# A hybrid encoder trunk on one core: four passes with one sequence's mixers laid between the other's feed-forward matmuls

## The chip, the core and the metric

The kernel runs on one core of one Trainium2 chip. Its metric is the device time in microseconds. TensorE does the matmuls and transposes, VectorE and ScalarE the elementwise work, and SyncE issues the DMAs; GpSimd has no part in it. Each engine works through its own list of instructions in order and waits on semaphores.

## The reference, cut to what matters

Two layers act on two sequences of 512 tokens of width 1024 (`x_prompt` and `x_sample`, with the same weights).

```
def encoder_layer(x, ...):
    h = rms_norm(x, norm_mix_g)
    proj = h @ w_in                       # 2864 columns
    aq, ak, av, bq, bk, bv, bg, ba, cq, ck, cv, co, cg = split(proj)
    attn = axial_gqa_attention(...)       # 8 heads of 64, 2 key heads, rotary, softmax over 512 keys
    gla = gla_mixer(...)                  # 4 heads, both directions, decay per channel
    mls = mlstm_mixer(...)                # 4 heads, both directions, gates with a running maximum
    x = x + concatenate([attn, gla, mls]) @ w_out
    u = centred_dwconv(rms_norm(x, norm_ffn_g) @ w_up, conv_w, conv_b)   # 3 taps over tokens, 5632 columns
    gate, val = split(u)
    return x + (silu(gate) * val) @ w_down                               # 2816 rows
```

## The kernel before, in words

Features lie on partitions and tokens on the free axis: `x` is [128, 8, 1024] for both sequences together. Every operand of a projection is split into a rounded part and its remainder (`whi` and `wlo`, `hh` and `hl`, `acth` and `actl`), and `passes3` (lines 433 to 435) issues three matmuls for each product. The dense work comes in units of weights of [128, 1024], 512 KB. SyncE loads a unit into `raw`, ScalarE writes `whi` (lines 820 and 1050), VectorE subtracts and writes `wlo` (lines 1149 and 1608). A unit serves both sequences.

One loop runs over the two layers. In a layer the stages follow each other:

- The norm: squares, their sum over partitions by a matmul with ones (line 417), root, reciprocal, the spreading over partitions (line 425), then eight rows for each sequence (`hf` line 1179, `hh` line 842, `hl` line 1183).
- The input projection of 23 units: 14 with tokens on the output's partitions (128x256 outputs), 9 with features there (128x512). Its results are moved by ScalarE and VectorE by turns, and rotary work of the queries and keys lies between.
- The mixers of both sequences. Queries and keys are split and transposed. In attention each of 64 steps has scores (lines 529 and 530), the row maximum (`nmx`, 1285), the exponential with its sum (906), four transposes (540), the copy of these (`pT`, by VectorE and ScalarE in turns, 1293 and 927), and the product with the values (551), with a hand-written shift of two and three steps. Three banks hold scores, three hold outputs, two hold transposes. The gates of linear attention (Abs, Exp, Ln; bias line 899) are put among the steps. Linear attention then goes chunk by chunk (32 tokens): states (582, 1472), scores (596), outputs (614, 620), with the backward direction's gates and the mLSTM's gate rows laid between its chunks. The mLSTM has 8 heads (4 for each sequence): row terms (669) in two banks, key-query products (678, 679) in four, decays (1008, 1012), products (1559), values (695) and a division (1526 to 1537).
- The output projection of 8 units, with `x` loaded back from memory, and then the second norm.
- The feed-forward: a loop over 22 tiles `j` of the inner width. For each, a gate unit and a value unit are multiplied for both sequences (96 matmuls of 128x512), ScalarE gives the middle tap with bias, VectorE adds the outer taps (1618, 1621), Silu and product (1075, 1645), split (1089, 1648), and the down unit of `j - 1` adds 16 products of 128x512 to `x` (line 1630).

```
                    pe.wait_ge(g_conv, j)
                    up(0, j)
                    pe.wait_ge(v_conv, j)
                    up(1, j)
                    down(j - 1, first=first)
```

The order of each engine's work is this written order alone; there is no planner. A mixer's memory shares regions with the weights' splits, with `hh` and `hl` and with `x`, so no mixer can run beside a projection.

## Time and profile before

| what | value |
| --- | --- |
| time, median of 3 runs | 3286.31 us (3283.18 to 3289.34) |
| span of the profiled execution, from first to last instruction | 3279.8 us |
| its device time beyond the span | not recorded apart; the median lies 6.5 us above the span |
| instructions | 41387 |
| mean granted TensorE clock | 0.907 of full speed |
| busy: TensorE, its weight loads, VectorE, ScalarE | 89%, 74%, 58%, 29% |

A share of busy time is an average over stages with different limits. Time in a stage is read from a window of the trace, and the clock column says at what part of full speed TensorE was let run there. The busy time of matmuls is modelled at its end, so the number of matmuls in a window is the firmer figure.

### The profile page before, as it was taken

To read this page: it belongs to the slowest core of one execution; us is meant where nothing else is said; L and a number is where in the kernel's file an instruction comes from. 1 tells how busy PE (TensorE), PEld (TensorE's weight loads), DVE (VectorE), ACT (ScalarE), POOL (GpSimd) and SP (SyncE) were. 2 spreads that over 40 slices of the span, in tenths; PEclk is the share of its full clock that TensorE was granted. 3 is DMA by queue.
4 is the path that set the end of the run, shared out by engine and by line. 5 is a ranking of instruction groups with operands and counts; after the bars stand their busy time and mean duration, and the time that the engine had idled before them with its cause. 6 is when DMAs were issued, how large, how long until landed. Compare 5 with 4: busy or idle time off the path is not lost.

```text
span 3279.8 us, 41387 instructions
## 1 busy us (share of the span) xinstructions
PE 2919.6 (89%) x16292; PEld 2435.9 (74%) x16292; DVE 1914.4 (58%) x2737; ACT 939.7 (29%) x1457; POOL 0.2 (0%) x4
## 2 busy tenths in 40 slices
PE   6999878778799999999889988797697999999997
PEld 6987766567688787878679867665676878788785
DVE  5532775664466666576646236756635675666666
ACT  3112641343222222222221145414323222222222
POOL 0000000000000000000000000000000000000000
PEclk9999985579899999999989999755698999999998
DMA  4110000002011111111121100000020111111111
GB/s 170 50 48 17 1 1 1 7 1 104 13 58 38 57 39 41 55 38 58 58 76 39 53 9 1 1 1 7 1 104 33 39 39 57 38 58 38 54 42 58
DMA packets 35624, 131.55 MB, mean 40 GB/s; under 512 B 4196, under 2 KB 5732, under 8 KB 35244
## 3 DMA queue, kind: packets, MB, share of 16 engines
q1 hardware_dynamic: 35500, 129.82, 11.3%
q8 instruction: 88, 1.44, 0.2%
q14 instruction: 36, 0.29, 0.0%
HBM read 117.22 MB, written 12.58 MB: 40 GB/s over the span
## 4 chain that ended last, share of the span: by engine, by line
PE 82%; DVE 10%; issue 4%; ACT 3%; DMA 1%; SPq 0%; DVEq 0%; ACTq 0%; PEldq 0%
PE ps L433 22%; PE ps L435 22%; PE ps L434 21%; PE ps L695 3%; PE ps L551 3%; PE ps L614 2%; PE ps L620 1%; DVE x L1630 1%; PE ps L582 1%; PE ps L540 1%; DVE sqsum L1120 1%; PE ps L678 1%; PE ps L529 1%; PE ps L679 1%; PE ps L530 1%
## 5 line engine op out<-in xcount | busy, mean ns | idle before, releaser
L433 PE MATMUL ps<-hh,wlo 128*128 128x512 f32 x1952 | 769.5, 394 | 61.0 <-PE ps L435 38.3
L435 PE MATMUL ps<-hh,whi 128*128 128x512 f32 x1952 | 762.0, 390 | 0.0
L434 PE MATMUL ps<-hl,whi 128*128 128x512 f32 x1952 | 761.6, 390 | 0.0
L1630 DVE TENSOR_TENSOR x<-x,ps 128x512 f32<-128x512 f32 x704 | 482.4, 688 | 284.9 <-PE ps L435 284.7
L433 PEld LDWEIGHTS ps<-hh,wlo 128*128 128x128 f32 x1952 | 367.3, 188 | 170.5 <-issue 94.0
L435 PEld LDWEIGHTS ps<-hh,whi 128*128 128x128 f32 x1952 | 367.4, 188 | 77.8
L434 PEld LDWEIGHTS ps<-hl,whi 128*128 128x128 f32 x1952 | 367.7, 188 | 73.6
L433 PE MATMUL ps<-acth,wlo 128*128 128x512 f32 x704 | 280.7, 399 | 17.0 <-DVE actl L1648 14.3
L435 PE MATMUL ps<-acth,whi 128*128 128x512 f32 x704 | 278.2, 395 | 0.0
L433 PE MATMUL ps<-whi,hl 128*128 128x256 f32 x896 | 256.6, 286 | 24.0 <-DVE wlo L1149 20.3
L434 PE MATMUL ps<-actl,whi 128*128 128x512 f32 x704 | 276.0, 392 | 0.0
L434 PE MATMUL ps<-wlo,hh 128*128 128x256 f32 x896 | 255.4, 285 | 0.0
L435 PE MATMUL ps<-whi,hh 128*128 128x256 f32 x896 | 255.3, 285 | 0.0
L1050 ACT ACTIVATE whi<-raw 128x1024 fp32r<-128x1024 f32 x132 | 138.7, 1054 | 398.2 <-PEq L757 380.8
L433 PEld LDWEIGHTS ps<-whi,hl 128*128 128x128 f32 x896 | 173.9, 194 | 28.5 <-DVE wlo L1149 22.7
L1618 DVE SCALAR_TENSOR_TENSOR accg<-ps,cw,accg 128x1022 f32<-128x1022 f32 x44 | 56.4, 1282 | 232.8 <-ACT accg L1068 232.8
L434 PEld LDWEIGHTS ps<-wlo,hh 128*128 128x128 f32 x896 | 173.9, 194 | 0.0
L435 PEld LDWEIGHTS ps<-whi,hh 128*128 128x128 f32 x896 | 173.8, 194 | 0.0
L433 PEld LDWEIGHTS ps<-acth,wlo 128*128 128x128 f32 x704 | 133.7, 190 | 47.4 <-issue 15.1
L1608 DVE TENSOR_TENSOR wlo<-raw,whi 128x1024 fp32r<-128x1024 f32 x132 | 160.5, 1217 | 11.6 <-ACT whi L1050 11.6
L551 PE MATMUL ps<-tokA,pT 128*128 128x64 f32 x1024 | 141.0, 283 | 27.2 <-ACT pT L927 27.1
L551 PEld LDWEIGHTS ps<-tokA,pT 128*128 128x128 f32 x1024 | 130.8, 200 | 36.5 <-ACT pT L927 33.7
(212 smaller groups left out, 3645.5 us busy)
## 6 DMA issues: line engine op xcount, KB each, us to landing
raw<-d_w_ffn SPq DMA_DIRECT2D x132, 512.0 KB, 4.9
raw<-d_w_units SPq DMA_DIRECT2D x62, 512.0 KB, 3.9
d_x_out<-x SPq DMA_DIRECT2D x24, 512.0 KB, 2.6
x<-d_x_out SPq DMA_DIRECT2D x2, 4096.0 KB, 13.6
x<-d_x_in SPq DMA_DIRECT2D x8, 512.0 KB, 7.8
mR<-d_sel SPq DMA_DIRECT2D x2, 400.0 KB
w2s<-d_w2p SPq DMA_DIRECT2D x2, 256.0 KB, 2.6
cmask<-d_chunkmask SPq DMA_DIRECT2D x1, 256.0 KB, 3.0
```

The costliest lines, as they stand in the source:

```text
L433: pe.matmul(out, stat[1], mov[0], start=first, stop=False)
L434: pe.matmul(out, stat[0], mov[1], start=False, stop=False)
L435: return pe.matmul(out, stat[0], mov[0], start=False, stop=last)
L529: pe.matmul(ps[:, 3 + i % 3, :], q, ks[:, 1, h // 4, keys], start=True, stop=False)
L530: pe.matmul(ps[:, 3 + i % 3, :], q, ks[:, 0, h // 4, keys], start=False, stop=True).then_inc(sc_ready, 1)
L551: mm = pe.matmul(ps[:, v % 3, 0:HD], pT[:, v % 2, kt, :], tokA[:, s * SB + kt, c0:c0 + HD], start=(kt == 0), stop=(kt == SB - 1))
L614: mm = pe.matmul(ps[:, bank, cols], attT[:, i % 2, h % 2, h // 2, :], gv[:, tt, h * HD:(h + 1) * HD], start=True, stop=False, skip_group_c ...
L695: mm = pe.matmul(ps[:, 6 + d, j * (HD + 1):(j + 1) * (HD + 1)], Dts[w % 2][:, d, i, j * P:(j + 1) * P], vaug[:, s * SB + i, h, :], start=( ...
L1050: act.activation(whi[:, kind, :, :], raw[:, kind, :].rearrange("p (k c) -> p k c", k=KT), ACT.Copy).then_inc(f_hi[kind], 1)
L1608: dve.tensor_tensor(wlo[:, kind, :, :], raw[:, kind, :].rearrange("p (k c) -> p k c", k=KT), whi[:, kind, :, :].bitcast(F32), ALU.subtract ...
L1618: dve.scalar_tensor_tensor(acc[:, :, 1:SEQ], ps[:, pair:pair + 2, 0:SEQ - 1], cw[:, taps:taps + 1], acc[:, :, 1:SEQ], ALU.mult, ALU.add).t ...
L1630: dve.tensor_tensor(xs, xs, ps[:, 4 + o % 2 * 2 + s, :], ALU.add).then_inc(d_done, 1)
```

## The change

The kernel is written anew around one sequence at a time. A *pass* is a layer of a sequence: passes 0 and 1 are layer 0 of the two sequences, 2 and 3 layer 1. Each pass has its own input projection (23 units), mixers, output projection (8 units) and feed-forward (66 units), and each unit is loaded and split anew in every pass; `whi` has four slots and `wlo` and `raw` six. The order is: norm of sequence 0; projection 0; mixers 0 alone; output projection 0; then for p = 1, 2, 3 the projection of p, the feed-forward of p - 1 with the mixers of p between its matmuls, and the output projection of p; last, norm and feed-forward of pass 3. The other norms lie beside projections: their squares, sum, root, spreading and rows are handed out over the units of an input projection, or over the eight units of the output projection of passes 1 and 2.

The feed-forward of a pass is a list of 132 slots. Up units have two slots of 12 matmuls, a pair of down units four slots of 12. All engines go through the same list, and `steps_after` puts one of 114 mixer steps behind nearly every slot, from slot 1 to slot 125. The feed-forward keeps to PSUM banks 0 to 3 and the mixers to 4 to 7. So attention has two banks of scores, one of transposes and one of outputs, and all copies of transposes are ScalarE's. The output of four query tiles is scaled by one operation. An mLSTM head has one bank for row terms and one for key-query products. Linear attention's states are formed as products of all chunks first, and then a chain of 30 operations for each direction on VectorE; both directions' outputs are added in PSUM. Silu is replaced by Tanh of half the argument, x(1 + tanh(x/2)), with the factor one half in the value's taps. Evacuations of the input projection are all ScalarE's. All loops over layers and tiles are unrolled.

```diff
-                def iteration(j, first=False):
-                    pe.wait_ge(g_conv, j)
-                    up(0, j)
-                    pe.wait_ge(v_conv, j)
-                    up(1, j)
-                    down(j - 1, first=first)
-                iteration(1, first=True)
-                with pe.Fori(2, FT) as j:
-                    iteration(j)
-                down(FT - 1, last=True)
...
+FF_SLOTS = []
+for _jj in range(FF_PAIRS + 1):
+    if _jj < FF_PAIRS:
+        FF_SLOTS += [("up", 2 * _jj, 0, 0), ("up", 2 * _jj, 0, 1), ("up", 2 * _jj, 1, 0), ("up", 2 * _jj, 1, 1)]
+    if _jj >= 1:
+        FF_SLOTS += [("down", _jj - 1, 0, o) for o in range(SB)]
+    if _jj < FF_PAIRS:
+        FF_SLOTS += [("up", 2 * _jj + 1, 0, 0), ("up", 2 * _jj + 1, 0, 1),
+                     ("up", 2 * _jj + 1, 1, 0), ("up", 2 * _jj + 1, 1, 1)]
...
+MIX_STEPS = [("qk", tt) for tt in range(SB + 1)]
+MIX_STEPS += [("att", i) for i in range(N_ATT + 3)]
...
+def steps_after(slot):
+    n = len(MIX_STEPS)
+    return MIX_STEPS[min(slot, MIX_SPAN) * n // MIX_SPAN:min(slot + 1, MIX_SPAN) * n // MIX_SPAN]
...
+            def feed_slot(f, n):
+                kind, j, which, half = FF_SLOTS[n]
+                hh, hl = R_at[f % NSEQ]["hh"], R_at[f % NSEQ]["hl"]
+                if kind == "up":
+                    u = UNIT_AT[("up", f, j, which)]
+                    if half == 0:
+                        pe.wait_ge(lo_ready, u + 1)
+                        if j == 0:
+                            pe.wait_ge(h_ready, h_count(f)[1])
+                            if f + 1 < N_PASS:
+                                pe.wait_ge(proj_evac, E_ALL * (f + 1) + 33 + which)
+                        else:
+                            pe.wait_ge((g_conv, v_conv)[which], FT * f + j)
+                    for k in range(half * 4, half * 4 + 4):
+                        mm3 = passes3(ps[:, which, :], (whi[:, HI[u], k, :], wlo[:, LO[u], k, :]),
+                                      (hh[:, k, :], hl[:, k, :]), k == 0, k == KT - 1)
+                    if half == 1:
+                        mm3.then_inc(up_done, 1)
+                else:
+                    if half == 0:
+                        pe.wait_ge(lo_ready, UNIT_AT[("down", f, 2 * j + 1, 2)] + 1)
+                        pe.wait_ge(actl_ready, FT * f + 2 * j + 2)
+                        if j == 0 and f + 1 < N_PASS:
+                            pe.wait_ge(proj_evac, E_ALL * (f + 2))
+                    for o in (2 * half, 2 * half + 1):
+                        if j or o >= 2:
+                            pe.wait_ge(d_done, FF_ADDS * f + KT * j + o - 1)
+                        for m in range(2):
+                            u = UNIT_AT[("down", f, 2 * j + m, 2)]
+                            mm3 = passes3(ps[:, 2 + o % 2, :], (whi[:, HI[u], o, :], wlo[:, LO[u], o, :]),
+                                          (acth[:, m, :], actl[:, m, :]), m == 0, m == 1)
+                        mm3.then_inc(d_psum, 1)
...
+            def attention(p, i):
+                rb, xb = R_at[p % NSEQ], X_at[p % NSEQ]
+                at = N_ATT * p
+                if i < N_ATT:
+                    h, qt = i // SB, i % SB
+                    if i == 0:
+                        pe.wait_ge(qkT_act, 2 * SB * (p + 1))
+                        pe.wait_ge(qkT_dve, SB * (p + 1))
+                        pe.wait_ge(z_taken, SB * (p + 1))
+                    if i >= 2:
+                        pe.wait_ge(prob_ready, at + i - 1)
+                    q = rb["qs"][:, h, qt * P:(qt + 1) * P]
+                    pe.matmul(ps[:, 4 + i % 2, :], q, rb["ks"][:, 1, h // 4, :], start=True, stop=False)
+                    pe.matmul(ps[:, 4 + i % 2, :], q, rb["ks"][:, 0, h // 4, :], start=False,
+                              stop=True).then_inc(sc_ready, 1)
+                if 2 <= i < N_ATT + 2:
+                    v = i - 2
+                    pe.wait_ge(prob_ready, at + v + 1)
+                    if v >= 1:
+                        pe.wait_ge(pT_ready, at + v)
+                    for kt in range(SB):
+                        tr = pe.transpose(ps[:, 6, kt * P:(kt + 1) * P], xb["prob"][:, v % 3, kt * P:(kt + 1) * P],
+                                          ident[:])
+                    tr.then_inc(pT_psum, 1)
+                if i >= 3:
+                    v = i - 3
+                    pe.wait_ge(pT_ready, at + v + 1)
+                    if v >= SB and v % SB == 0:
+                        pe.wait_ge(ao_done, AH * p + v // SB)
+                    c0 = AV + v // SB // 4 * HD
+                    for kt in range(SB):
+                        mm = pe.matmul(ps[:, 7, v % 4 * HD:(v % 4 + 1) * HD], xb["pT"][:, v % 2, kt, :],
+                                       tokA[:, kt, c0:c0 + HD], start=(kt == 0), stop=(kt == SB - 1))
+                    mm.then_inc(ao_psum, 1)
...
+                if i >= 2:
+                    kt = i - 2
+                    pe.wait_ge(stk_lo, 3 * (at + w + 1))
+                    if w or kt:
+                        pe.wait_ge(wt_ready, 8 * (at + w) + 2 * kt)
+                    k = xb["ks2"][:, w % 2, kt * P:(kt + 1) * P]
+                    pe.matmul(ps[:, 5, :], k, xb["ql2"][:, w % 2, :], start=True, stop=False)
+                    pe.matmul(ps[:, 5, :], k, xb["qh2"][:, w % 2, :], start=False, stop=True).then_inc(qk_psum, 1)
...
+            for p in range(N_PASS):
+                q = side_norm(p, "in")[0]
+                for i in range(N_IN):
+                    if i == 6:
+                        sum_squares(q)
+                    if i == 10:
+                        spread(q)
+                    project(p, i)
+                if p == 0:
+                    for step in MIX_STEPS:
+                        mix_step(p, step)
+                else:
+                    for n in range(len(FF_SLOTS)):
+                        feed_slot(p - 1, n)
+                        for step in steps_after(n):
+                            mix_step(p, step)
+                beside = side_norm(p, "out")
...
+                    split_to(first + (3 if kind == "up" else 3))
+                if kind == "up" and half == 1:
+                    at = FT * f + j
+                    act.wait_ge(up_done, FF_UPS * f + 2 * j + which + 1)
+                    if which == 0:
+                        if at:
+                            act.wait_ge(act_ready, at)
+                        act.activation(accg[:], ps[:, 0, :], ACT.Identity, bias=convs[:, l, j, 3:4],
+                                       scale=convs[:, l, j, 1:2]).then_inc(g_init, 1)
+                        act.wait_ge(g_conv, at + 1)
+                        act.activation(sil[:], accg[:], ACT.Tanh, scale=0.5).then_inc(sil_ready, 1)
+                    else:
+                        if at:
+                            act.wait_ge(actl_ready, at)
+                        act.activation(accv[:], ps[:, 1, :], ACT.Identity, bias=convs[:, l, j, 7:8],
+                                       scale=convs[:, l, j, 5:6]).then_inc(v_init, 1)
+                        if j % 2 or j == 0:
+                            round_act(f, j)
+                if kind == "down" and half == 3 and j + 1 < FF_PAIRS:
+                    round_act(f, 2 * j + 2)
+            def round_act(f, j):
+                act.wait_ge(act_ready, FT * f + j + 1)
+                if j >= 2 or f:
+                    act.wait_ge(d_psum, FF_ADDS * f + KT * (j // 2))
+                act.activation(acth[:, j % 2, :], accv[:], ACT.Copy).then_inc(acth_ready, 1)
...
+            def attention(p, i):
+                rb, xb = R_at[p % NSEQ], X_at[p % NSEQ]
+                at = N_ATT * p
+                if i < N_ATT:
+                    act.wait_ge(nmx_ready, at + i + 1)
+                    if i >= 3:
+                        act.wait_ge(pT_psum, at + i - 2)
+                    act.activation(xb["prob"][:, i % 3, :], ps[:, 4 + i % 2, :], ACT.Exp, bias=nmx[:, i:i + 1],
+                                   accum_out=rsum[:, i:i + 1]).then_inc(prob_ready, 1)
+                if 2 <= i < N_ATT + 2:
+                    v = i - 2
+                    act.wait_ge(pT_psum, at + v + 1)
+                    if v >= 2:
+                        act.wait_ge(ao_psum, at + v - 1)
+                    act.activation(xb["pT"][:, v % 2, :, :].rearrange("p k q -> p (k q)"), ps[:, 6, :], ACT.Copy)\
+                       .then_inc(pT_ready, 1)
...
+            def feed_slot(f, n):
+                kind, j, which, half = FF_SLOTS[n]
+                l = f // NSEQ
+                x = X_at[f % NSEQ]["x"]
+                if half == 0:
+                    first = UNIT_AT[("up", f, j, which) if kind == "up" else ("down", f, 2 * j, 2)]
+                    split_to(first + 3)
+                if kind == "up" and half == 1:
+                    at = FT * f + j
+                    if which == 0:
+                        conv(accg, 0, convs[:, l, j, 0:4], g_init, g_conv, at)
+                    else:
+                        conv(accv, 1, convs[:, l, j, 4:8], v_init, v_conv, at)
+                        dve.wait_ge(sil_ready, at + 1)
+                        link(dve.scalar_tensor_tensor(accg[:], sil[:], 1.0, accg[:], ALU.add, ALU.mult))
+                        dve.wait_ge(v_conv, at + 1)
+                        dve.tensor_tensor(accv[:], accg[:], accv[:], ALU.mult).then_inc(act_ready, 1)
+                        if j % 2 or j == 0:
+                            rest_of_act(f, j)
+                if kind == "down":
+                    for o in (2 * half, 2 * half + 1):
+                        dve.wait_ge(d_psum, FF_ADDS * f + KT * j + o + 1)
+                        dve.tensor_tensor(x[:, o, :], x[:, o, :], ps[:, 2 + o % 2, :], ALU.add).then_inc(d_done, 1)
+                    if half == 3 and j + 1 < FF_PAIRS:
+                        rest_of_act(f, 2 * j + 2)
+            def rest_of_act(f, j):
+                dve.wait_ge(acth_ready, FT * f + j + 1)
+                dve.tensor_tensor(actl[:, j % 2, :], accv[:], acth[:, j % 2, :].bitcast(F32), ALU.subtract)\
+                   .then_inc(actl_ready, 1)
...
+                for m in (range(8) if part == 0 else range(8, 15)):
+                    c = m if d == 0 else NCH - 1 - m
+                    for hp in range(2):
+                        own = ps[:, 4 + c % 4, (c // 4 * 2 + hp) * HD:(c // 4 * 2 + hp + 1) * HD]
+                        if m == 0:
+                            ins = dve.tensor_copy(st[:, hp, c, :], own)
+                        else:
+                            dve.wait_ge(state_ready, at + 2 * m + hp - 1)
+                            before = c - 1 if d == 0 else c + 1
+                            ins = dve.scalar_tensor_tensor(st[:, hp, c, :], st[:, hp, before, :],
+                                                           aL[:, d, hp, c:c + 1], own, ALU.mult, ALU.add)
+                        ins.then_inc(state_ready, 1)
...
+                        dve.wait_ge(dt_ready, 8 * (at + w))
+                    dve.tensor_tensor(xb["mR"][:, d, :].rearrange("p (j t) -> p j t", j=SB),
+                                      ps[:, 4, :].rearrange("p (j t) -> p j t", j=SB),
+                                      mmask[:, d:d + 1, :].to_broadcast([P, SB, P]), ALU.add).then_inc(mr_ready, 1)
+                if w < MH and i == 2 and w + 1 < MH:
+                    stack_lo(p, w + 1)
+                if w >= 1 and i == (2 if w < MH else 1):
+                    divide(p, w - 1)
+                if i >= 2:
+                    kt = i - 2
+                    Dt = R_at[p % NSEQ]["Dt"][w % 2]
+                    dve.wait_ge(qk_psum, SB * (at + w) + kt + 1)
+                    for d in range(2):
+                        lo, hi = fwd_or_bwd_range(d, kt)
+                        dve.wait_ge(rb_used, 2 * (at + w + 1))
+                        dve.wait_ge(dt_ready, 8 * (at + w) + 2 * kt + d + 1)
+                        D_t = Dt[:, kt, decay_at(d, lo, hi)]
+                        dve.scalar_tensor_tensor(D_t, ps[:, 5, lo:hi], HD ** -0.5, D_t, ALU.mult,
+                                                 ALU.mult).then_inc(wt_ready, 1)
```

In the diff the first functions `feed_slot`, `attention` and the end of `mlstm_head` are TensorE's; the next `feed_slot` with `round_act` and `attention` are ScalarE's; the last ones VectorE's. `stack_lo` writes the three remainders of the next head, `divide` is the division of the head before. ScalarE splits the unit three ahead at the first half of a slot's unit, and VectorE does so too.

## Rows read from the trace of the kernel before

**Rows 1.** The page: busy time of TensorE and others, then its clock in 40 slices.

```profile
...
PE 2919.6 (89%) x16292; PEld 2435.9 (74%) x16292; DVE 1914.4 (58%) x2737; ACT 939.7 (29%) x1457; POOL 0.2 (0%) x4
...
PEclk9999985579899999999989999755698999999998
...
```

**Rows 2.** Windows: length, busy us of PE, PEld, DVE, ACT, POOL, clock, DMA, GB/s.

```profile
...
0.00:34.50 34.50, 6.94 (x20) 4.66 (x20) 16.80 (x21) 14.94 (x16) 0.20 (x4) 0.94 0.80 303
34.50:304.90 270.40, 265.74 (x1776) 244.58 (x1776) 105.70 (x140) 46.10 (x72) 0.00 (x0) 0.99 0.14 47
304.90:763.00 458.10, 352.72 (x2780) 294.24 (x2781) 302.53 (x598) 210.76 (x429) 0.00 (x0) 0.74 0.01 4
329.50:470.00 140.50, 125.79 (x896) 111.84 (x896) 97.00 (x236) 82.88 (x179) 0.00 (x0) 0.95 0.00 1
470.00:624.00 154.00, 117.44 (x1280) 90.33 (x1280) 96.12 (x141) 33.18 (x38) 0.00 (x0) 0.51 0.00 1
655.00:661.60 6.60, 5.36 (x17) 4.51 (x18) 6.50 (x14) 2.42 (x7) 0.00 (x0) 0.50 0.00 0
763.00:851.50 88.50, 86.49 (x374) 69.15 (x372) 22.48 (x21) 12.91 (x13) 0.00 (x0) 1.00 0.23 90
851.50:896.40 44.90, 28.79 (x116) 21.07 (x117) 32.67 (x43) 17.18 (x25) 0.00 (x0) 0.86 0.07 24
900.00:1600.00 700.00, 685.18 (x2985) 558.77 (x2984) 446.61 (x511) 158.00 (x166) 0.00 (x0) 1.00 0.13 46
...
```

**Rows 3.** Timeline of TensorE in one attention step: start, us, instruction.

```profile
...
384.56 0.48 PE L529 MATMUL ps<-ks,qs 128*128 128x512 f32 x1
...
385.11 0.60 PE L540 MATMUL ps<-ident,prob 128*128 128x128 f32 x4
...
386.36 0.48 PE L529 MATMUL ps<-ks,qs 128*128 128x512 f32 x1
...
```

**Rows 4.** Groups of the feed-forward and norms, by shape: busy us, mean ns, idle before.

```profile
...
L1630 DVE TENSOR_TENSOR x<-x,ps 128x512 f32<-128x512 f32 x704 | 482.4, 688 | 284.9 <-PE ps L435 284.7
...
L1608 DVE TENSOR_TENSOR wlo<-raw,whi 128x1024 fp32r<-128x1024 f32 x132 | 160.5, 1217 | 11.6 <-ACT whi L1050 11.6
...
L1050 ACT ACTIVATE whi<-raw 128x1024 fp32r<-128x1024 f32 x132 | 138.7, 1054 | 398.2 <-PEq L757 380.8 <-DMA raw<-d_w_ffn 16.6
...
L1179 DVE SCALAR_TENSOR_TENSOR hf<-x,vec,ps 128x512 f32<-128x512 f32 x64 | 47.1, 746 | 16.8 <-DMA vec<-d_vecs 9.0 <-PE ps L425 6.2
...
L842 ACT ACTIVATE hh<-hf 128x512 fp32r<-128x512 f32 x64 | 40.5, 632 | 71.1 <-DVE hf L1179 70.9
...
L899 ACT ACTIVATE G<-ps,vec 128x512 f32<-128x512 f32 x16 | 11.0, 689 | 4.7 <-PE ps L497 4.7
...
```

**Rows 5.** Groups of the attention steps, by shape.

```profile
...
L906 ACT ACTIVATE prob<-ps,nmx 128x512 f32<-128x512 f32 x128 | 87.9, 687 | 108.8 <-DVE nmx L1285 108.7
...
L927 ACT ACTIVATE pT<-ps 128x512 f32<-128x512 f32 x64 | 37.7, 588 | 3.3 <-PE ps L540 3.3
L1319 DVE TENSOR_SCALAR tokA<-ps,rinvp 128x64 f32<-128x64 f32 x128 | 36.3, 283 | 66.9 <-PE ps L551 62.6 <-DVE rinvp L1296 0.9
...
L906 ACT ACTIVATION_READ_ACCUMULATOR prob<-ps,nmx 128x1 f32 x128 | 24.8, 194 | 0.0
...
L906 ACT ACT_TABLE_LOAD x6 | 7.7, 1283 | 0.1
...
```

**Rows 6.** Timeline of an mLSTM head: start, us, instruction, idle before and its releaser.

```profile
...
656.24 0.76 PE L678 MATMUL ps<-ql,ks 128*128 128x512 f32 x1 [3.05 <-DVE Dt L1559]
...
665.31 0.17 DVE L1526 COPY dn<-ps 128x8 f32<-128x8 f32 x1 [3.59 <-PE ps L695]
...
667.34 0.42 DVE L1537 TENSOR_TENSOR co<-co,hs 128x256 f32<-128x256 f32 x1
...
672.18 4.57 PE L695 MATMUL ps<-vaug,Dt 128*128 128x65 f32 x40
...
```

2420 lines of the change are left out of this document (1158 added, 1262 removed).

## The prediction

> **What bounds the kernel now.** I read the page first. TensorE is busy for 89% of the span and its granted clock is full or nearly so but for one stretch in each layer [rows 1]. So I cut one layer into stages [rows 2]: the input projection, 270.4 us, the mixers, 458.1, the output projection, 88.5, the norm before the feed-forward with its first loads, 44.9, and 700 us of the feed-forward. Its 3168 matmuls at the 700/2985 us of that row are 743, so of half the span, 1640, some 80 are left for norms. What the reader is to see is the clock column. Projections and feed-forward hold 0.99 to 1.00 with TensorE busy for 98% of the time; there only fewer matmuls could help. The mixers hold 0.74 on average, and the gated-linear-attention stretch 0.51. So 458 us a layer, 916 in all, run without the dense matmuls, and the norms are 160 more. That is all that overlap can win from.
>
> **What the change does to each part.** Matmuls of the projections and of the feed-forward keep their number. The change works on one sequence of 512 at a time, in four passes. Mixers of passes 1 to 3 lie beside the feed-forward of the pass before; those of pass 0, one norm and the last feed-forward stay alone. The price is twofold: each weight unit is loaded and split four times, not twice (388 for 194), and all engines now run one common list of 132 slots with 114 mixer steps laid in, each engine in order.
>
> *Loads.* 194 more units of 512 KB add some 100 MB to 130 over the whole run; the feed-forward moves 46 GB/s now and the start 303 [rows 2]. The ring loads five or six units ahead, so I cost it at nothing. Splits: 194 times 1.05 us on ScalarE and 1.22 us on VectorE [rows 4]. In the projections they lie beside matmuls. Beside mixers they don't, see below.
>
> *Start to dense projection*: 34.5 now [rows 2]; half the squares, but each of 8 rows of the norm paces the first tile: 32. *Projections*: four passes of half the row, 4 x 135.2 = 541. *Output projections*: 4 x 44.25, and 1 us each for the last adds: 181. *Last norm*, for one sequence: 8 squares summed (8 x 0.69), root and spreading (some 6), 8 rows of two VectorE operations of 0.69 to 0.75: 25, of 44.9 now.
>
> *Mixers of pass 0, alone.* Half of 458 would be 229. But the new list has one bank where there were three or several, so chains are serial. Attention: a score needs the probability two steps before, whose copy comes behind an exponential on ScalarE: 0.69 + 0.19 + 0.59 (ScalarE), 1.3 (transposes and values on TensorE), 0.7 (scores), 0.69 (maximum, VectorE's price for 512 columns) for two steps, 4.3 with handovers, 2.15 each as now (140.5/64) [rows 2 to 5]: 35 steps 75, gates 10. Query and key transposes 21. Linear attention 85 (half of the row is 77, the rest is its single chain). Norms and gate rows 29, that were laid in it before. mLSTM heads 19 each, 76: splits, division and the first products stand one behind another on VectorE. Last norm and mix 12. Together 308.
>
> *One slot of the passes 1 to 3.* Twelve 128x512 matmuls at 685.18/2985 = 0.23 us [rows 2] are 2.75 us; 132 slots 363. Mixers add per sequence: attention 1.80 a step (384.56 to 386.36 [rows 3]), 32 of them 58; heads 4 x 7 = 28 (40 matmuls of values 4.57 [rows 6]); linear attention some 35 (half of 117.44, which ran at clock 0.51); the rest 16: 137. The bound from the other side is half of the 352.7 us that the mixers were busy, 176 [rows 2]. TensorE's floor for a pass is thus 500 us. VectorE: 66 splits of 1.22, 88 adds of 0.69, 88 convolution steps of 0.75, 66 products and remainders of 0.69 [rows 4]: 252, and half the mixers' 302.5 is 151 [rows 2]: 403. So neither engine is full; what costs is order.
>
> *The waits, by chain.* (a) At the end of an odd value unit VectorE and ScalarE must do, in this order: bias 0.69, two convolutions 1.5, two products 1.4, rounding 0.63, remainder 0.69, then the maximum 0.69, exponential with its sum 0.88, and the copy 0.59 [rows 4, 5]. With 0.05 for each of nine handovers, 0.16 from the slot's last issue to the matmul's end (my estimate), and ScalarE 0.4 late from the step before, that is 8.1 us after the slot's matmuls. TensorE gets to the transposes that need this copy after 1.80 + 2.75 + 0.55 = 5.1. It waits 3.0. (b) After an even value unit the same chain without rounding: 1.2. (c) The adds of the down projection stand behind (b) and a split; its third product needs the first add: 1.5, and 3.1 where no mixer step lies between. Over the twelve slots of two j: 12 x 4.55 = 54.6 and 5.7 of waits, 60.3, 5.0 a slot. (d) In the heads, step 2 puts on VectorE a split 1.22, the next head's remainders 3 x 0.69, the division 2.45 (665.31 to 667.76) and the first products 1.0, behind a ScalarE that is late itself; TensorE's next key-query product has one bank and needs them [rows 6]. I get 6 to 7 us of idle per head, and 31.5 per head against 23.5 of matmuls. In the kernel before the like of it is seen once a head, 3.05 idle [rows 6].
>
> *The clock.* That idle time of 3.05 at 653 to 656 is followed by a granted clock of 0.50 from 655.0 to 661.6 [rows 2, 6]: the next matmuls run at 1.2 GHz, not 2.4. Waits (a), (d) and the 3.1 of (c) are as long. I take 2 us for each; in the feed-forward of before there were no such waits, and it held 1.00.
>
> *Sum of a pass's slots*: queries and keys 5 slots, serial, 38; attention 35 x 5.0 + 4 empty slots 11 + gates and scans 8 + clock 2 = 196; preparation and state chains, 26 slots, 104 (VectorE 84 and its waits, in lumps of 8 us: 60 operations of 0.28 [rows 5]); output tiles 5 slots, 43; norms and gate rows 13 slots, 45; heads 4 x 31.5 + 2 more steps 8 + 3 empty slots 8 + clock 4 = 146; last norm and mix 35; the 7 other slots with the last activation's chain 27. Sum 634, 134 over the floor. Both ends: no wait at all, 500; all waits half as long again and a slower clock after each, 690.
>
> *Last feed-forward*: 363, ten waits (c) of 3.1 and their clock 2 each, 51, first and last chain and store 11: 425. (Before, half of 743: 372.)
>
> Total: 32 + 541 + 308 + 181 + 3 x 634 + 25 + 425 = 3414, against a span of 3279.8. The median of the runs lies 6.5 us above that span; with it, 3420. The removed 916 of mixers and 160 of norms come back as 308, 25, three times 271 of mixer matmuls and waits, and 62 in the last feed-forward, 1208 in all.
>
> For Tanh, which takes the place of Silu beside the exponentials, no row shows which functions share a table; I add no load. The Trainium skill (ScalarE: Activation LUTs, "Table sets: the hidden batching unit") lists tanh in the set of exp, which would keep these loads away; no run here shows it yet.
>
> **Rivals.**
> 1. *The streams interleave cleanly (faster).* ScalarE and VectorE have 30% and more of idle time in a pass, and where a wait is long the engines behind catch up. With fixed parts of 1512 the kernel is faster once a pass's slots take under (3280 - 1512)/3 = 589 us, so if the waits are under 89 rather than 134. At 530 it gives 3110. For it: in the feed-forward of before VectorE was busy for 64% and TensorE lost only 2% [rows 2]. Against: the heads before waited 3 us each, with more banks.
> 2. *A clock that never settles (much slower).* The mixers' windows at 0.51 and 0.74 have shown that many small matmuls with idle time between hold the clock low [rows 2]. If the slots see a clock of 0.85, a pass takes 690: 3590. Against: the attention stretch, busy for 90%, held 0.95.
> 3. *Tanh and Exp each load a table.* A load is 1.28 us [rows 5]; two for each of 22 units in 3 passes are 170 us of ScalarE, on chain (a): some 120 more, 3540. A profile with some 130 more loads would show it.
> 4. *Nothing comes of it*: the gain of the overlap and the price of waits and splits cancel, 3280.
>
> The Trainium skill describes rival 2 (TensorE: Matmul & The Clock Gate, "A second HAM failure mode: psum-queue depth-cycling"): short idle times at each change of PSUM banks make the clock swing, even in dense kernels. By it also the 1 us waits would tell. The trace agrees only for the 3 us ones: from 900 to 1600 us, with a bank handover in every unit, it is 1.00.
>
> **Chances.** Forecast 0.56, rival 1 0.22, rival 2 0.12, rival 3 0.06, rival 4 0.04. A difference of 0.2% is about what a measurement can tell here. Faster 0.22, same 0.04, slower 0.74. Time 3420; the likeliest case alone reaches from 3330 to 3500. The range takes in half of rival 1 and the near part of rival 2: 3180 to 3580.
>
> **What would show it.** Right: 400 or so splits of each kind; TensorE's busy share down to about 80% or less outside the projections; idle of about 3 us before the probability transposes once in two j, of 5 and more before the key-query products, both released by VectorE or ScalarE; clock 0.9 to 0.95 in the slots; each pass's slots 590 to 690 us; pass 0's mixers about 308 us. Wrong: slots under 589 us with waits of 1 us and less (rival 1), or pass 0's mixers near 230, so that my serial chains are too long; a clock near 0.85; table loads in the hundreds.

## Result and the profile after

The changed kernel takes **3430.93 us** (median, 3430.12 to 3435.4), the kernel before 3287.82 beside it: a ratio of 1.0447, interval 1.0429 to 1.0464. It is 143 us slower. The forecast was 3420.

The page of the changed kernel has these lines in answer to [rows 1], and the chain that ended last:

```profile
span 3429.1 us, 39998 instructions
...
PE 2888.8 (84%) x16272; PEld 2398.8 (70%) x16272; DVE 1892.1 (55%) x2821; ACT 1260.2 (37%) x2014; POOL 0.2 (0%) x4
...
PEclk9985579999988899989989899999999889899999
...
PE 66%; DVE 19%; ACT 9%; issue 5%; DMA 0%; SPq 0%; ACTq 0%; DVEq 0%
...
```

Subtract busy TensorE time from each span. Before, 3279.8 - 2919.6 leaves 360 us in which TensorE did nothing; now it is 3429.1 - 2888.8 = 540. Busy time fell by 31, although the number of matmuls is nearly the same. The two dips of the clock to 0.5 to 0.7 of [rows 1] have become one, but the rest now shows 8 beside 9, and the mean granted clock is 0.904 for 0.907, so the clock as a whole won nothing. By shape, matmuls of the down units got longer (450, 428 and 424 ns each for 399, 392 and 395), and two kinds of linear attention got shorter (the 256 with `attT` 322 ns for 447, the state products 252 for 316). How much of that is the clock and how much the new form of these products was not separated. So the change won 31 us of busy time and paid 180 in idle time.

Windows of the changed kernel, with the columns of [rows 2]: the mixers of pass 0 alone, seven parts of pass 1's slots, the whole slots of passes 1, 2 and 3, and the last feed-forward.

```profile
...
162.00:471.00 309.00, 191.07 (x1384) 154.88 (x1384) 132.15 (x268) 125.34 (x246) 0.00 (x0) 0.65 0.02 6
...
644.40:692.00 47.60, 33.12 (x142) 25.44 (x141) 16.85 (x24) 19.59 (x32) 0.00 (x0) 0.82 0.13 44
692.00:874.00 182.00, 168.99 (x885) 141.95 (x884) 99.92 (x140) 85.73 (x149) 0.00 (x0) 0.94 0.15 53
874.00:990.00 116.00, 92.14 (x633) 72.89 (x632) 80.67 (x147) 39.19 (x50) 0.00 (x0) 0.90 0.20 68
990.00:1026.00 36.00, 36.00 (x410) 28.89 (x411) 15.67 (x22) 3.68 (x6) 0.00 (x0) 0.91 0.09 31
1026.00:1092.00 66.00, 43.04 (x192) 33.47 (x190) 39.89 (x54) 28.77 (x37) 0.00 (x0) 0.90 0.16 56
1092.00:1240.00 148.00, 122.69 (x555) 100.06 (x554) 86.38 (x144) 52.95 (x101) 0.00 (x0) 0.88 0.15 51
1240.00:1292.00 52.00, 40.67 (x171) 32.38 (x169) 32.71 (x48) 17.16 (x27) 0.00 (x0) 0.87 0.26 90
644.40:1292.00 647.60, 536.65 (x2968) 435.09 (x2966) 372.09 (x576) 247.07 (x400) 0.00 (x0) 0.90 0.16 57
1473.00:2115.00 642.00, 530.57 (x2968) 430.11 (x2967) 372.55 (x576) 247.43 (x400) 0.00 (x0) 0.91 0.17 57
2296.00:2941.00 645.00, 533.33 (x2967) 432.37 (x2965) 372.65 (x576) 247.13 (x400) 0.00 (x0) 0.90 0.16 57
3012.00:3429.00 417.00, 381.09 (x1578) 307.83 (x1576) 241.50 (x304) 122.18 (x151) 0.00 (x0) 0.95 0.24 81
...
```

A pass's slots last 642 to 648 us. VectorE works for 372 of them and ScalarE for 247: neither is near full, and TensorE still idles for 111.

What TensorE waited for in the whole run (us in total, times, longest):

```profile
PE ps L439 <- DVE x L1273: 109.7, 34, 14.8
PE ps L697 <- DVE Dt L1516: 88.9, 30, 8.1
PE ps L596 <- DVE t1g L1348: 75.4, 8, 10.9
PE ps L543 <- DVE kd L1297: 47.4, 10, 7.7
PE ps L572 <- ACT pT L898: 40.1, 33, 3.4
...
```

Four of the five are released by VectorE: the add of the down projection, the weighting of a head's products, the scaled keys of linear attention, the low half of the keys. A VectorE that is half idle and still late points at the order of its work. The longest wait shows it. This is the timeline of the changed kernel before the matmul at 1893.29 (start, duration; in brackets the idle time before and its releaser):

```profile
1881.23 1.28 ACT L978 ACT_TABLE_LOAD   x1
1882.53 0.72 ACT L978 ACTIVATE fl<-fl,ones 36x512 f32<-36x512 f32 x1
1883.16 1.04 ACT L799 ACTIVATE whi<-raw 128x1024 fp32r<-128x1024 f32 x1
...
1884.30 1.22 DVE L1165 TENSOR_TENSOR wlo<-raw,whi 128x1024 fp32r<-128x1024 f32 x1 [4.48 <-ACT whi L799]
...
1887.60 0.68 DVE L1265 SCALAR_TENSOR_TENSOR accg<-sil,accg 128x512 f32<-128x512 f32 x1
1888.32 0.69 DVE L1267 TENSOR_TENSOR accv<-accg,accv 128x512 f32<-128x512 f32 x1
1888.93 1.21 DVE L1451 TENSOR_TENSOR_SCAN Fc<-ones,fl 4x512 f32<-4x512 f32 x1
1890.17 1.21 DVE L1453 TENSOR_TENSOR_SCAN mm_rows<-fl,ri 4x512 f32<-4x512 f32 x1
1891.42 1.23 DVE L1165 TENSOR_TENSOR wlo<-raw,whi 128x1024 fp32r<-128x1024 f32 x1
1892.56 1.28 DVE L1273 TENSOR_TENSOR x<-x,ps 128x512 f32<-128x512 f32 x2
1893.29 0.29 PEld L439 LDWEIGHTS ps<-acth,wlo 128*128 128x128 f32 x1 [15.12 <-DVE x L1273]
...
```

VectorE stood idle for 4.48 us, because ScalarE's rounding of a weight unit stood behind a table load and a gate row. Then it worked without a pause from 1884.30 to 1893.8. TensorE wanted the first add of the last line but one. Ahead of it in the program stood a split for a unit three ahead, two products of an activation that is needed only in the next pair, and two scans for heads that come later. Nothing here is too much work; it is the urgent operation standing last.

### The profile page after: what moved, and what is told of

Read it like the earlier page. It is cut to its first block, busy times and chain, and to the rows that moved or that the text cites. A ratio compares the mean times of both kernels' runs of the same rounds, so it can differ in the third digit from the quotient of the medians.

```text
span 3429.1 us, 39998 instructions
## 1 busy us (share of the span) xinstructions
PE 2888.8 (84%) x16272; PEld 2398.8 (70%) x16272; DVE 1892.1 (55%) x2821; ACT 1260.2 (37%) x2014; POOL 0.2 (0%) x4
## 4 chain that ended last, share of the span: by engine, by line
PE 66%; DVE 19%; ACT 9%; issue 5%; DMA 0%; SPq 0%; ACTq 0%; DVEq 0%
PE ps L439 18%; PE ps L441 17%; PE ps L440 17%; DVE wlo L1165 3%; PE ps L582 2%; PE ps L686 2%; ACT whi L799 2%; DVE accv L1246 1%; DVE accv L1248 1%; ACT accv L848 1%; PE ps L640 1%; DVE st L1396 1%; PE ps L572 1%; DVE accg L1265 1%; DVE accv L1267 1%
## 5 line engine op out<-in xcount | busy, mean ns | idle before, releaser
L439 PE MATMUL ps<-hh,wlo 128*128 128x512 f32 x1952 | 800.3, 410 | 24.3 <-DVE hl L1197 11.4
L1165 DVE TENSOR_TENSOR wlo<-raw,whi 128x1024 fp32r<-128x1024 f32 x388 | 468.5, 1223 | 495.8 <-ACT whi L799 493.2
L799 ACT ACTIVATE whi<-raw 128x1024 fp32r<-128x1024 f32 x388 | 399.8, 1050 | 153.1 <-PE ps L441 152.8
L439 PE MATMUL ps<-acth,wlo 128*128 128x512 f32 x704 | 316.8, 450 | 132.4 <-DVE x L1273 107.1
L1273 DVE TENSOR_TENSOR x<-x,ps 128x512 f32<-128x512 f32 x352 | 238.5, 686 | 297.0 <-PE ps L441 296.6
L440 PE MATMUL ps<-actl,whi 128*128 128x512 f32 x704 | 301.0, 428 | 0.0
L441 PE MATMUL ps<-acth,whi 128*128 128x512 f32 x704 | 298.8, 424 | 0.0
L860 ACT ACTIVATE acth<-accv 128x512 fp32r<-128x512 f32 x88 | 55.5, 631 | 406.0 <-PE ps L441 265.4
L441 PEld LDWEIGHTS ps<-acth,whi 128*128 128x128 f32 x704 | 148.5, 211 | 36.4
L440 PEld LDWEIGHTS ps<-actl,whi 128*128 128x128 f32 x704 | 150.2, 213 | 30.3
```

Source lines behind the costliest of these rows:

```text
L439: pe.matmul(out, stat[1], mov[0], start=first, stop=False)
L440: pe.matmul(out, stat[0], mov[1], start=False, stop=False)
L441: return pe.matmul(out, stat[0], mov[0], start=False, stop=end)
L799: act.activation(whi[:, HI[m], :, :], raw[:, LO[m], :, :], ACT.Copy)\
L860: act.activation(acth[:, j % 2, :], accv[:], ACT.Copy).then_inc(acth_ready, 1)
L1165: dve.tensor_tensor(wlo[:, LO[m], :, :], raw[:, LO[m], :, :], whi[:, HI[m], :, :].bitcast(F32), ALU.subtract).then_inc(lo_ready, 1)
```

## Experiments

All are edits of the changed kernel. The differences from it are of medians; the kernel before had medians of 3287.0 to 3292.4 beside them. "Idle" is the span less TensorE's busy time, from each page.

| kernel | us | against before (interval) | against changed | idle | clock |
|---|---|---|---|---|---|
| changed | 3430.9 | 1.0447 (1.0429 to 1.0464) | | 540 | 0.904 |
| e6 serial | 3667.4 | 1.1151 (1.1133 to 1.117) | +237 | 654 | 0.852 |
| e1 copy first | 3395.8 | 1.0343 (1.0314 to 1.0373) | -35 | 515 | 0.907 |
| e2 head spread | 3409.3 | 1.0363 (1.0346 to 1.038) | -22 | 515 | 0.904 |
| e3 states | 3433.0 | 1.045 (1.0432 to 1.0467) | +2 | 534 | 0.899 |
| e5 adds first | 3376.9 | 1.027 (1.0253 to 1.0287) | -54 | 508 | 0.910 |
| e11 products only | 3312.5 | 1.0056 (1.0039 to 1.0073) | -118 | 464 | 0.918 |
| e7 double low half | 3654.6 | 1.1118 (1.1099 to 1.1136) | +224 | 699 | 0.878 |
| e8 Silu | 3466.0 | 1.0522 (1.0505 to 1.054) | +35 | 562 | 0.902 |
| e9 = e1+e2+e3+e5 | 3275.5 | 0.9963 (0.9951 to 0.9975) | -155 | 425 | 0.922 |
| e10 = e9+e11 | 3194.9 | 0.9731 (0.9715 to 0.9747) | -236 | 356 | 0.929 |
| e12 = e10 without e3 | 3230.7 | 0.9814 (0.9797 to 0.983) | -200 | 396 | 0.925 |
| e13 = e10 + late key transposes | 3149.5 | 0.9571 (0.9555 to 0.9587) | -281 | 329 | 0.935 |

By the bound of 2% that is used here, e9 and e11 are the same as the kernel before, e12 is unclear, and e10 and e13 are faster. The pages and windows of e11 come from its longest run, with a span of 3318.6 us: beside them the gain is 110.5 us and not 118.

**What the overlap is worth (e6).** All mixer steps stand behind the last slot of the feed-forward.

```diff
-    return MIX_STEPS[min(slot, MIX_SPAN) * n // MIX_SPAN:min(slot + 1, MIX_SPAN) * n // MIX_SPAN]
+    return MIX_STEPS if slot == len(FF_SLOTS) - 1 else []
```

> All 114 mixer steps of passes 1 to 3 come behind the last slot of the feed-forward, none between its matmuls. This tells what laying them between is worth. Theory (overlap works in part): a pass's slots then take 414 of feed-forward and 309 of mixers, 723 instead of 645, so 3431 + 3 x 78 = 3665, between 3620 and 3700. Rival (waits eat the whole overlap, and the doubled splits are the loss): 3431 within 30 us. Second rival (the clock in dense stretches gains): 3550.

Measured: 3667.4. Windows of this kernel, a feed-forward alone and its mixers alone:

```profile
644.00:1064.00 420.00, 384.79 (x1597) 310.50 (x1595) 246.83 (x310) 128.10 (x161) 0.00 (x0) 0.95 0.23 83
1064.00:1370.00 306.00, 190.85 (x1389) 155.18 (x1390) 134.20 (x270) 123.89 (x243) 0.00 (x0) 0.65 0.04 13
...
```

420 + 306 = 726 where the interleaved slots take 645. So interleaving itself wins some 80 us a pass. The change is slower because its parts are slower than before's: 306 for mixers of one sequence, against half of 458 [rows 2], and 420 for a feed-forward, against half of the 743 of the prediction.

These figures close the account, as an estimate. Four mixers and four feed-forwards of one sequence, one behind the other, are 4 x (306 + 420) = 2904 us, where the kernel before has 916 + 1486 = 2402: 502 more. Laying three pairs together takes off 3 x 81 = 243. The start and the norms take 57 where they took 160, because most of them now lie beside projections: 103 less. The projections are 712 for 718. What is left is 150, and the spans differ by 149. So the overlap worked, and the working in single sequences cost more than it gave.

**The copy of the probabilities first (e1).** In a step ScalarE copies the transposes that are done before it takes the exponential of the next scores.

```diff
-                if i < N_ATT:
...
-                    act.activation(xb["prob"][:, i % 3, :], ps[:, 4 + i % 2, :], ACT.Exp, bias=nmx[:, i:i + 1],
-                                   accum_out=rsum[:, i:i + 1]).then_inc(prob_ready, 1)
                 if 2 <= i < N_ATT + 2:
...
                     act.activation(xb["pT"][:, v % 2, :, :].rearrange("p k q -> p (k q)"), ps[:, 6, :], ACT.Copy)\
                        .then_inc(pT_ready, 1)
+                if i < N_ATT:
...
+                    act.activation(xb["prob"][:, i % 3, :], ps[:, 4 + i % 2, :], ACT.Exp, bias=nmx[:, i:i + 1],
+                                   accum_out=rsum[:, i:i + 1]).then_inc(prob_ready, 1)
```

> ScalarE copies the transposed probabilities of two steps before first, and computes this step's exponential after it; nothing else changes. Theory (the written order on the engines makes the waits): TensorE's wait for this copy stood behind the maximum and the exponential. In the changed kernel it waits 27.8 us for it in passes 1 to 3, with slower matmuls after some of these waits, and in pass 0 the serial loop of an attention step loses most of an exponential every two steps (35 steps, 0.3 us each). Together 25 to 45 us less than 3431. Rival (whatever is late, the next thing in the list is as late): under 10 us of change. Second rival: the exponential now stands behind the transposes and comes late itself, slower by up to 20 us.

Measured -35, as the theory said. The wait for pT fell from 40.1 to 4.7 us. The add's total rose from 109.7 to 120.1: part of the wait was handed on.

**The head's lump spread (e2).** The next head's remainders go to the end of step 3 and the division of the head before to the end of step 4, both behind the products of the step.

```diff
-                if w < MH and i == 2 and w + 1 < MH:
-                    stack_lo(p, w + 1)
-                if w >= 1 and i == (2 if w < MH else 1):
+                if w == MH and i == 1:
                     divide(p, w - 1)
...
+                if i == 3 and w + 1 < MH:
+                    stack_lo(p, w + 1)
+                if i == 4 and w >= 1:
+                    divide(p, w - 1)
```

> In an mLSTM head VectorE does its two products first in each step; the next head's three remainders go to the end of step 3, the division of the head before to the end of step 4 (both stood ahead of the first products in step 2). Theory: the lump of 4.5 us in one step makes the idle of up to 8.1 us before the key-query product; passes 1 to 3 wait 63 us there in 18 waits, and pass 0 some 15. 35 to 60 us less than 3431. Rival (VectorE has too much to do in the heads, wherever it stands): under 15 us less, and the waits reappear one step on.

Measured -22, between the theory (35 and more) and the rival (under 15). The wait for Dt fell from 88.9 to 52.0 us but not in number, and the add's rose to 119.1.

**Adds before the split (e5).** In the first slot of a pair of down units VectorE's two adds stand ahead of its split.

```diff
-                if half == 0:
-                    first = UNIT_AT[("up", f, j, which) if kind == "up" else ("down", f, 2 * j, 2)]
+                if half == 0 and kind == "up":
+                    first = UNIT_AT["up", f, j, which]
                     split_to(first + 3)
...
                         dve.tensor_tensor(x[:, o, :], x[:, o, :], ps[:, 2 + o % 2, :], ALU.add).then_inc(d_done, 1)
+                    if half == 0:
+                        split_to(UNIT_AT["down", f, 2 * j, 2] + 3)
```

> At the first half slot of each down pair VectorE adds its two outputs to x first and then makes the remainder of a unit; the order was the reverse. Theory: TensorE's third product waits for the first add, so the split of 1.22 us is on its path 44 times. With what the clock loses after waits of 3 us: 45 to 80 us less than 3431, 15 to 25 of it in the last feed-forward, which took 417. Rival (the adds are late for the products of the activation alone, or the split is now late): under 15 us.

Measured -54. In its list of waits:

```profile
PE ps L439 <- DVE x L1273: 76.0, 25, 13.6
...
```

34 us less wait there, and the clock went from 0.904 to 0.910. Nothing else in the list moved by more than 2.

**States in five steps, transposes a step later (e3).** The second direction is changed like the first; the last lines are of TensorE's `gla_prep`, its transposes of the scaled keys.

```diff
-              ("prep", 1, 0), ("kv", 0, 2), ("prep", 1, 1), ("kv", 0, 3), ("chain", 0, 0), ("chain", 0, 1),
+              ("prep", 1, 0), ("kv", 0, 2), ("prep", 1, 1), ("kv", 0, 3)] + [("chain", 0, i) for i in range(5)] + [
...
-                for m in (range(8) if part == 0 else range(8, 15)):
+                for m in range(3 * part, 3 * part + 3):
...
-                if i == 2:
+                if i == 3:
```

> Edit: the state chain of each direction is laid in five steps of three chunks instead of two of eight and seven, and TensorE's transposes of the scaled keys come one step later than the step in which VectorE makes them. Theory: these lumps are waits of TensorE's own program (the transposes wait 75.4 us and the state matmuls 33 us over the run, of which 58 and 11 us in the slots), so most of that goes and the run takes 40 to 80 us less than the changed kernel, 3350 to 3390. Rival one, the wait is only handed to the next wait of the same group (the attention's value chain or the adds): under 15 us less, 3416 to 3431. Rival two, ten steps instead of four dilute the other steps and more small waits lie between: slower by up to 15 us.

Measured +2: the theory fell. The number lies just above rival one's range (up to 3431) and within rival two's (up to 15 slower); the list of waits of this kernel speaks for rival one:

```profile
PE ps L439 <- DVE x L1273: 146.0, 40, 13.3
...
PE ps L596 <- DVE t1g L1348: 38.6, 5, 9.8
...
```

The transposes' wait fell by 37 as meant, and the add's rose by 36. That the one was handed to the other is read from these totals; e12 below tests it.

**VectorE's order at the end of a value unit (e11).** The two products, the rounding and the remainder of an activation stood at the end of the value unit. Now an even unit's products stand behind the second slot of the down units, and an odd unit's whole group in the first slot of the next gate unit. `products` holds the four removed lines; ScalarE's rounding moves in the same way.

```diff
+                late = kind == "up" and half == 0 and which == 0 and j >= 2 and j % 2 == 0
+                if late:
+                    products(f, j - 1)
                 if half == 0:
...
                     split_to(first + 3)
+                if late:
+                    rest_of_act(f, j - 1)
...
-                        dve.wait_ge(sil_ready, at + 1)
-                        link(dve.scalar_tensor_tensor(accg[:], sil[:], 1.0, accg[:], ALU.add, ALU.mult))
-                        dve.wait_ge(v_conv, at + 1)
-                        dve.tensor_tensor(accv[:], accg[:], accv[:], ALU.mult).then_inc(act_ready, 1)
-                        if j % 2 or j == 0:
+                        if j == 0 or j == FT - 1:
+                            products(f, j)
                             rest_of_act(f, j)
                 if kind == "down":
...
+                    if half == 1 and j + 1 < FF_PAIRS:
+                        products(f, 2 * j + 2)
```

> Edit: of the five reorderings only the last, made on the changed kernel: the activation's two products, rounding and remainder stand behind the second half-slot of the down matmuls (even unit) or in the first half-slot of the next gate unit (odd unit) instead of at the end of the value unit. Beside the kernel with all four others it took 80 us (3275 to 3195). Theory, the prediction's chain (a) behind the odd value unit is the largest lump of VectorE's order, so it gives the same alone: 60 to 90 us less than the changed kernel, 3340 to 3370. Rival, the gain needs the others: less than 40 us, above 3390.

Measured -118, outside the theory's 60 to 90 and the largest of all single edits. Its windows, the slots of pass 2 (in the changed kernel 642.00) and the last feed-forward (417.00):

```profile
1444.00:2059.00 615.00, 523.35 (x2962) 426.51 (x2961) 372.10 (x577) 248.28 (x401) 0.00 (x0) 0.92 0.17 60
...
2927.00:3318.00 391.00, 368.90 (x1576) 295.93 (x1574) 239.61 (x304) 122.17 (x151) 0.00 (x0) 0.99 0.24 86
...
```

27 us in pass 2 and 26 in a feed-forward in which no mixer runs. VectorE's work in pass 2 is the same to 0.5 us. In its list of waits no single entry carries it:

```profile
PE ps L439 <- DVE x L1277: 94.3, 40, 13.4
PE ps L697 <- DVE Dt L1529: 78.8, 27, 6.1
PE ps L596 <- DVE t1g L1361: 64.0, 8, 9.7
...
PE ps L572 <- ACT pT L900: 15.2, 18, 3.1
...
```

Four waits are shorter by 15, 10, 11 and 25: whatever stands behind the value unit comes earlier. By the pages, idle time is 76 us less and busy time 34.5 less, at a clock of 0.918. In the last feed-forward the clock is 0.99 where it was 0.95, and there single waits can be followed. TensorE waits ten times for the add, 27.3 us in the changed kernel and 14.0 in e11. This is one of the ten with the 6 us behind it, first of the changed kernel, then of e11:

```profile
3235.90 0.80 PE L439 MATMUL ps<-acth,wlo 128*128 128x512 f32 x1 [2.73 <-DVE x L1273]
...
3235.90:3241.90 6.00, 6.00 (x19) 4.88 (x20) 1.92 (x4) 0.00 (x0) 0.00 (x0) 0.72 0.00 0
...
```

```profile
3206.84 0.50 PE L439 MATMUL ps<-acth,wlo 128*128 128x512 f32 x1 [1.40 <-DVE x L1277]
...
3206.80:3212.80 6.00, 5.96 (x25) 4.67 (x26) 4.04 (x7) 0.00 (x0) 0.00 (x0) 1.00 0.00 0
...
```

Nine of the ten waits of 2.73 us were followed by a clock of 0.72 to 0.74 over 6 us (the first by 1.00); all ten of 1.40 to 1.43 us by 1.00. So of the 26 us, 13.3 are shorter waits and 12.2 are matmuls that no longer run slowly.

**What the doubled splits cost (e7).** After each low half VectorE takes the maximum of it with itself.

```diff
-                                      whi[:, HI[m], :, :].bitcast(F32), ALU.subtract).then_inc(lo_ready, 1)
+                                      whi[:, HI[m], :, :].bitcast(F32), ALU.subtract).then_inc(again, 1)
+                    dve.wait_ge(again, m + 1)
+                    dve.tensor_tensor(wlo[:, LO[m], :, :], wlo[:, LO[m], :, :].bitcast(F32),
+                                      wlo[:, LO[m], :, :].bitcast(F32), ALU.max).then_inc(lo_ready, 1)
```

> Edit: after each low half of a weight unit VectorE does a second pass over the same 1,024 columns, the maximum of the low half with itself, before TensorE may use it; values are the same. That is 388 more VectorE instructions, some 470 us of VectorE work by the 1223 ns of the low half. Question: how much of the weight splits' VectorE time lies on TensorE's path. The kernel before splits half as many units (each is used for both sequences), so half of this price, 194 units, is what the doubled splits cost the change on VectorE. Theory (VectorE takes its work in program order and mixers, adds and value chains stand behind the splits): 80 to 180 us more, 3510 to 3610, so the doubled splits explain 40 to 90 us. Rival one, the splits lie in VectorE's idle time: at most 30 us more, below 3461. Rival two, they are the whole loss: over 240 us more.

Measured +224, above the theory's range and just under rival two. Its group of VectorE:

```profile
L1169 DVE TENSOR_TENSOR wlo<-wlo 128x1024 fp32r<-128x1024 f32 x388 | 475.3, 1225 | 13.3
...
```

475 us of added work, 229 us more span. In a pass's slots 66 more such operations are 81 us of work, and the window of pass 2's slots, 642.00 in the changed kernel, shows

```profile
1537.50:2247.50 710.00, 558.07 (x2982) 451.00 (x2981) 455.87 (x647) 247.82 (x402) 0.00 (x0) 0.87 0.16 53
...
```

68 more. From the first transposes of the queries to the last ones behind the mixers, which needs no choice of a window, pass 2 takes 665.8 us for 603.8, 62 more. So between matmuls about four fifths of a new VectorE operation lie on the path, though VectorE is busy for 58% there in the changed kernel. In the last feed-forward, where no mixer runs, it is half: 456 us for 417. Ahead of pass 1's slots it is nothing: the 54 units of the first three projections bring 66 us of such work, and the first transposes of pass 1 start at 652.6 us, in the changed kernel at 654.6. The change made 194 more splits. Half of 224, 112 us, is my estimate of what they cost on VectorE. It takes the price as proportional, which wasn't tried, and the edit also hands each low half over 1.2 us later, which the change's own splits don't.

**Table loads (e8).** ScalarE's `ACT.Tanh` of the gate becomes `ACT.Silu`; the gate's values differ.

> Edit: in the changed kernel ScalarE's function of the gate is Silu with the same scale instead of Tanh, so the activation's values differ; everything else stands. It tests the prediction's rival 3, table loads between the interleaved streams. Theory, Tanh shares a table with the mixers' exponential and Silu does not, so between a gate unit and the next attention or head step there are two loads: 60 to 130 more of them at 1283 ns, and the kernel takes 40 to 130 us more, 3470 to 3560. Rival one, ScalarE (37 per cent busy) hides them: under 20 us. Rival two, the number of loads stays at some 60 because the step already mixes sets: no change.

Measured +35. ScalarE's loads at that line and at the exponential's, first of the changed kernel, then of this one:

```profile
L844 ACT ACT_TABLE_LOAD x13 | 16.7, 1283 | 0.2
L891 ACT ACT_TABLE_LOAD x9 | 11.5, 1283 | 0.2
...
```

```profile
L844 ACT ACT_TABLE_LOAD x58 | 74.4, 1283 | 1.1
L891 ACT ACT_TABLE_LOAD x27 | 34.6, 1283 | 0.5
...
```

In all 90 more ScalarE instructions, 2104 for 2014, and 117.5 us more busy time; 35 of it reach the span. Much of the rest took the place of idle time: ahead of the gate's function ScalarE waited 162.4 us for the convolution in the changed kernel and waits 103.3 here. The number came as the theory said, the price stayed just below its range.

**Four edits together (e9).**

> Edit: the copy of the probabilities before the exponential, the products of a head before its two lumps, the states and late transposes, and the adds before the split, all in one kernel. Theory, they take away waits of different places and add up: 35, 22 and 54 us measured alone plus what the states give (40 to 80): 150 to 190 us less, 3240 to 3280, on the fast side of the kernel before. Rival, they compete for the same slack, since a wait shortened moves VectorE's next lump nearer: 60 to 70 per cent of the sum, 3300 to 3340, and the change stays slower.

Measured 3275.5, at the slow end of the theory's range. Alone the four gave 109 us; together they give 155.

**All five (e10).**

> Edit: the kernel with all four reorderings, and the activation's two products, its rounding and its remainder taken out of the end of the value unit: for an even unit they stand behind the second half-slot of the down matmuls, for an odd one in the first half-slot of the next gate unit. Theory, behind an odd value unit a chain of split, convolution, two products and remainder (8.1 us in the prediction) still holds up the mixer step, so spreading it takes another 25 to 60 us: 3190 to 3250. Rival, without the lump that stood there the steps are covered already, and the later products hold up the down matmuls instead: within 10 us of the kernel with all four or slower.

Measured 3194.9, in the theory's range, 80 us from e9.

**All but the states (e12).**

> Edit: the kernel with all five reorderings, without the spread states and the late transposes, which alone gave nothing (3433 beside 3431). Theory one, in the third experiment the waits that it took away (some 40 us at the transposes) came back at the adds, because more steps pushed mixer work between split and adds; with the adds ahead of the split they don't, so leaving it out costs 20 to 50 us: 3215 to 3245. Theory two, it never gave anything and the other four were worth more together than alone for another reason (the clock): within 8 us of 3195.

Measured 3230.7: theory one. With the states spread (e10 against e12) the wait of the transposes is 36.3 us for 64.0, and the add's doesn't rise this time: 68.9 for 73.0. The edit that gave nothing alone is worth 36 us here. On the changed kernel it led from 3430.9 to 3433.0, beside the other four from 3230.7 to 3194.9.

**The key transposes a step later (e13).** On top of e10, TensorE makes the transposes of a token tile one step after ScalarE and VectorE make its halves.

```diff
-                if tt == SB:
+                tt -= 1
+                if tt < 0:
                     return
```

> Edit: the fastest kernel so far (all five reorderings, the states and late transposes among them; 3195 us), and TensorE makes the transposes of queries and keys of a token tile, and its gate matmul, one step after the step in which ScalarE and VectorE make their high and low halves, so that a half-slot of feed-forward matmuls lies between. Theory: the waits of these transposes for the low half (47.4 us in ten) go in the slots, of which 37 us lie there: 20 to 40 us less, 3155 to 3175, some 3.5 per cent below the kernel before. Rival, the evacuation of the transposes in the same step then waits and VectorE's adds behind it are late: under 10 us less, above 3185.

Measured 3149.5, 45 us less, a little more than the theory's range: the fastest kernel, 4.3% below the kernel before. Against e10, idle time is 27 us less and busy time 16; the wait itself fell by 23, so the theory's place is right and part of the gain came with the clock. Lines of its page, windows of its pass 2 and last feed-forward, and two of its waits:

```profile
span 3147.4 us, 39998 instructions
...
PE 2818.2 (90%) x16272; PEld 2347.6 (75%) x16272; DVE 1880.6 (60%) x2821; ACT 1265.2 (40%) x2014; POOL 0.2 (0%) x4
...
PEclk9986569999999999999999999999999999899999
...
```

```profile
1380.00:1951.00 571.00, 517.03 (x2984) 420.64 (x2983) 372.49 (x580) 252.09 (x404) 0.00 (x0) 0.96 0.19 66
...
2768.00:3147.00 379.00, 368.01 (x1571) 294.88 (x1570) 239.67 (x304) 122.16 (x151) 0.00 (x0) 0.99 0.25 89
...
```

```profile
PE ps L439 <- DVE x L1278: 69.1, 49, 7.8
...
PE ps L544 <- DVE kd L1313: 24.3, 10, 2.8
...
```

The instructions are those of the changed kernel, 39998, in another order. Of 282 us of span, 211 are idle time of TensorE and 71 the clock of the same 16272 matmuls. Of the 329 us that are still idle, 106 lie in the mixers of pass 0, which nothing covers: 298 us, 192 busy, at a clock of 0.62.

## Why the prediction was right, point by point

*The whole.* Forecast 3420, measured 3430.9. The sum itself was 3414 against a span of 3429, 15 off. The 6.5 us that were added for the time beyond the span are 1.8 in this run (3430.87 against 3429.1); in all runs listed with a span it is 1.7 to 2.1. The 6.5 set a median beside the span of another execution. By term (forecast, measured):

| term | forecast | measured |
|---|---|---|
| start | 32 | 31 |
| four input projections | 541 | 525 |
| mixers of pass 0 alone | 308 | 309 |
| four output projections | 181 | 187 |
| slots of passes 1 to 3 | 3 x 634 | 648 + 642 + 645 |
| last norm | 25 | 26 |
| last feed-forward | 425 | 417 |

The projections' 525 is what the other windows leave of 3429.

*Serial chains of pass 0.* Right, to a microsecond in 309. The transposes of queries and keys end near 185 us and attention near 270, so these two took 21 and 85 us, as forecast. The clock of 0.65 is 0.92 up to there and 0.50 to 0.54 from there to the last head. The prediction's reason for serial chains was that the mixers have fewer banks than before; no run gave them more, so that isn't shown.

*TensorE's floor and the waits.* 500 and 134 were forecast, pass 2 shows 531 busy and 111 idle. The 500 are matmuls at full clock, and the slots were granted 0.90 to 0.91; in e13, at 0.96, the same matmuls are busy for 517. The forecast had 6 us for the clock in a pass (2 in attention, 4 in the heads), the slots show some 31 (531 less the 500, an estimate), and its waits, 128 without these 6, came as 111. The two misses cancel, so that the sum is right to within 14 us is in part luck.

*Inside a pass, sizes compensate.* In pass 1 attention was sized at 196 and took 182; queries and keys 38 and 48; preparation and state chains 104 and 116; output tiles 43 and 36; norms and gate rows 45 and 66; heads 146 and 148; the last steps with the empty slots 62 and 52. Three have a reason that a trace shows. In attention chain (a) does end in the wait for the pT copy in each of the three pairs of pass 1, with 3.4, 2.1 and 0.9 us beside 3.0 forecast; chain (b) gives 0.7, 1.4 and 0.7 beside 1.2, and the adds 1.2 to 1.3 beside 1.5. In the queries the chain was longer than counted: its two waits are 12.5 us in pass 2, and e13, which puts a slot between, wins 45 over the run. In the gate rows I saw small operations and not that they stand ahead of a split and of adds; that one wait of 14.7 us is the timeline above, and it is of the size of most of the 21 missing.

*Chain (a) was right about the place and too narrow about the reach.* The prediction charged the lump at the end of a value unit to attention and, in chain (c), to the adds. Moving it (e11) shortens the waits of the heads by 10 us and those of linear attention by 11 as well, and gives 118 us in all. So a time of most of the change's loss comes back without removing an operation. That isn't a share of the 143: by e7 the doubled splits are an estimated 112, and the two together are more than the 143.

*Chain (c)*: without mixers ten waits of 3.1 us were forecast, with 2 us of slow matmuls behind each. The last feed-forward shows ten of 2.7, and by e11 some 1.2 of slow matmuls for each. e5, which puts the adds ahead of the split, takes away 54 us over the run. *Chain (d)*: heads at 148 for 146, as forecast, Dt's waits up to 8.1 us. The idle time of their window, 25 us, is 6.3 a head, where 6 to 7 were forecast. e2 takes 37 of the 89 us of Dt's waits away.

*The clock*, forecast at 0.9 to 0.95 in the slots, is 0.90 to 0.91. The prediction held that waits of 3 us cost it and those of 1 us don't. In the last feed-forward that came so: nine of ten waits of 2.7 us were followed by a fall, none of those of 1.4 in e11. Between mixers it was too kind: in pass 1 waits of 1.38 and 1.25 us that lie 2.7 us apart (782.81 and 785.52) were followed by 0.75 over 6 us. Two pairs of 0.7 and 1.2 us were followed once by 0.72 (843.19) and once by 1.00 (725.75), so the length of a wait alone doesn't tell it. That the prediction left these out fits the clock term that came too small. Over the run e11 against the changed kernel gives 34.5 us of busy time for 76 of idle time, so 0.45 us of slower matmuls for each us waited.

*Splits.* The prediction said that they lie beside matmuls in the projections and that beside mixers they don't. e7 shows both: nothing ahead of pass 1's slots, four fifths in them. By e7 they are an estimated 112 us; the forecast had them inside its chains and gave them no number of their own.

*Rivals.* The second, a clock of 0.85, didn't come; e6, with bare mixers in each pass, shows it: 0.852 and 3667. The third, a table load for each of two functions, is refuted for Tanh: 13 loads at its line for 88 uses. By the Trainium skill ("ScalarE: Activation LUTs", "Table sets: the hidden batching unit") tanh is in the set of exp, and the trace agrees. With Silu 90 loads come and cost 35 us, so the rival's price was too high too: 120 for 130 loads, where this rate gives 51. The first, a clean interleave below 589 us a pass, isn't the changed kernel; e13, at 571, gets there by order alone. The bound itself was good: with the measured fixed parts, 3429.1 - 1934.6 = 1494.5, it is (3279.8 - 1494.5)/3 = 595. The fourth, no difference, didn't come.

*Signs.* Those named for the forecast came, one of them weakly: the splits are 388 of each kind; TensorE is busy for about 80% outside the projections (2888.8 less some 700 of the 712 us of projections, in the 2717 left; an estimate); the slots' length, their clock and pass 0's mixers are in their ranges. Of the idle stretches before the key-query products, 5 us and more appears once in pass 1 (8.1), the others are 1.3 to 4.7, and before the probability transposes 3 us came in one of three pairs.

*What stays open.* Why the four edits give 46 us more together than alone is shown only in part: leaving out the states costs 36 us with the four other edits there and nothing on the changed kernel. Which pair of the others helps each other wasn't tried. What the smaller number of banks costs the mixers wasn't tried either. That half of the splits' measured price is the price of doubling is an estimate. The wait of 24 us for the first gate rows in pass 0 and the 298 us of its mixers weren't touched.

## What to carry to other kernels

When two streams are laid into one program for engines that work in order, the sum of an engine's work doesn't tell the loss; what stands ahead of the operation that the matmuls wait for does. Here VectorE was at 55%, and still 475 us of added work cost 224, while moving four operations of each activation gave 118. Read the timeline ahead of the longest wait and ask of each operation there who needs it next; move those that nobody needs behind the one that releases TensorE. Judge such edits in company: a wait that is removed is often handed to the next one in the list, and the edit that gave nothing alone gave 36 us once the wait that received its gain was gone.

## What the runs showed of the hardware that I had not expected

- A wait of 2.7 us cost its clock and one of 1.4 didn't. In the last feed-forward of the changed kernel nine of ten waits of 2.73 us were followed by a granted clock of 0.72 to 0.74 over 6 us, with the first 2 us of it at 0.50 to 0.51, the lower level of 1.2 GHz: 381 us busy at 0.95. In e11 the ten waits of 1.40 to 1.43 us were followed by 1.00, and the same matmuls are busy for 369 at 0.99. Between mixers shorter waits close together could cost it too: 1.38 and 1.25 us, 2.7 us apart, were followed by 0.75. The Trainium skill ("TensorE: Matmul & The Clock Gate", "A second HAM failure mode: psum-queue depth-cycling") says that short idle times at bank changes swing the clock. The traces agree for the waits of 2.7 us and for some pairs of shorter ones, and not for single ones of 1.4.
- Silu in place of Tanh brings 45 more table loads at the gate's line and 18 at the exponential's, each 1283 ns, as every load in these traces; of 117.5 us more on ScalarE 35 are seen in the span, at a ScalarE busy for 40%.
